# First attention of a two-block transformer kernel: each unit's transpositions placed ahead of the preceding unit's values on TensorE

## What is computed

```python
# "a": sparse attention, 8 heads of 64, 2 key/value heads; the keys of a query are chosen by an indexer
dots   = einsum('bqhd,bsd->bqhs', q_index, k_index)
iscore = einsum('bqh,bqhs->bqs', w_index, relu(dots))      # masked to the past, top 64 keys kept
p      = softmax(q_a @ k_a.T * scale, masked to the chosen keys);  o_a = p @ v_a
# "b": latent attention, 8 heads of 64 + 32 query/key features, 64 value features, causal
p      = softmax((q_nope @ k_nope.T + q_rope @ k_rope.T) * scale, masked);  o_b = p @ v_b
merged = sigmoid(g_a) * (o_a @ w_branch_a) + sigmoid(g_b) * (o_b @ w_branch_b)
h      = h + merged @ w_out
```

## Time and profile before

| | |
|---|---|
| three runs | 999.68, 1000.36, 1000.6 us; median 1000.36 us |
| the profiled execution | 999.73 us, of which 997.9 us are the span of the profile |
| granted TensorE clock over the span | 0.998 |
| busy, share of the span | PE 98%, weight loads 84%, DVE 68%, ACT 54%, POOL 4% |
| the chain that ended last | PE 76%, issue 19%, DVE 2%, others 1% each or less |
| first attention | units 0 to 15 from about 79.5 to 155.3 us |

### The profile page before, as it was taken

One profiled execution on the slowest core, in us unless ns is written; L12 is line 12 of the kernel. 1 busy time (PEld: TensorE's weight loads), 2 busy tenths in 40 slices (PEclk: granted clock), 3 DMA queues, 4 the chain that ended last, 5 costly groups with the idle time before them and its releaser, 6 DMA issues.

```text
span 997.9 us, 15646 instructions
## 1 busy us (share of the span) xinstructions
PE 981.6 (98%) x6349; PEld 841.6 (84%) x6349; DVE 677.7 (68%) x831; ACT 542.8 (54%) x708; POOL 42.9 (4%) x68
## 2 busy tenths in 40 slices
PE   7999999999999999999999999999999999999997
PEld 6887777898888888887889888888899898888885
DVE  5689787688777787777767565656656566555564
ACT  6676664476555565634445444444555455444452
POOL 1210000000000005000000000000000000000000
PEclk9999999999999999999999999999999999999999
DMA  8354335466656555844347565656553446656541
GB/s 306 103 192 158 109 120 178 161 211 211 209 170 209 171 168 164 261 146 155 120 133 259 188 207 190 204 185 201 185 168 133 155 142 214 207 172 207 174 163 43
DMA packets 121283, 175.89 MB, mean 176 GB/s; under 512 B 3167, under 2 KB 89770, under 8 KB 121226
## 3 DMA queue, kind: packets, MB, share of 16 engines
q1 hardware_dynamic: 118860, 168.82, 51.0%
q0 software_dynamic: 1600, 5.09, 1.6%
q10 hardware_dynamic: 766, 1.16, 0.5%
HBM read 173.82 MB, written 1.25 MB: 175 GB/s over the span
## 4 chain that ended last, share of the span: by engine, by line
PE 76%; issue 19%; DVE 2%; DMA 1%; ACT 1%; POOL 1%; SPq 0%; POOLq 0%; DVEq 0%; ACTq 0%
PE ps L1851 22%; PE ps L1901 16%; PE ps L1872 10%; PE ps L1900 7%; PE ps L1888 5%; PE ps L1915 3%; PE ps L1923 2%; DMA raw<-in_w_in 1%; PE ps L2141 1%; PE ps L2336 1%; PE ps L1903 1%; PE ps L1966 1%; PE ps L2169 1%; PE ps L2397 1%; PE ps L1997 1%
## 5 line engine op out<-in xcount | busy, mean ns | idle before, releaser
L1090 DVE TENSOR_TENSOR w_lo<-raw,w_hi 128x2048 fp32r<-128x2048 f32 (+3 forms) x153 | 345.3, 2261 | 125.2 <-ACT w_hi L548 124.9
L1901 PE MATMUL ps<-x_both,w_hi 128*128 128x512 f32 x992 | 342.7, 396 | 0.0
L548 ACT ACTIVATE w_hi<-raw 128x2048 fp32r<-128x2048 f32 (+3 forms) x161 | 302.4, 1879 | 58.9 <-PE ps L1851 40.1
L1900 PE MATMUL ps<-x_both,w_lo 128*128 128x256 f32 x868 | 242.0, 279 | 0.0
L1901 PEld LDWEIGHTS ps<-x_both,w_hi 128*128 128x128 f32 x992 | 179.1, 188 | 34.5
L1900 PEld LDWEIGHTS ps<-x_both,w_lo 128*128 128x128 f32 x868 | 163.6, 189 | 5.5
L803 ACT ACTIVATE work<-ps 128x512 f32<-128x512 f32 x66 | 39.3, 596 | 150.2 <-PE ps L1901 134.4
L1851 PE MATMUL ps<-w_hi,x_both 128*128 128x512 f32 (+1 forms) x320 | 101.5, 387 | 0.3 <-DVE w_lo L1090 0.3
L1851 PE MATMUL ps<-w_hi,hid_hi 128*128 128x512 f32 x240 | 93.8, 391 | 0.0
L1851 PE MATMUL ps<-w_hi,hid_lo 128*128 128x512 f32 x240 | 93.4, 389 | 0.0
L1851 PE MATMUL ps<-w_lo,hid_hi 128*128 128x512 f32 x240 | 93.4, 389 | 0.0
(11 more groups left out here) (294 smaller groups left out, 1274.2 us busy)
## 6 DMA issues: line engine op xcount, KB each, us to landing
raw<-in_ffn_w SPq DMA_DIRECT2D x66, 1024.0 KB, 5.1
raw<-in_w_up SPq DMA_DIRECT2D x22, 1024.0 KB, 5.1
raw<-in_hgrn_w_in SPq DMA_DIRECT2D x16, 1024.0 KB, 5.5
raw<-in_w_in SPq DMA_DIRECT2D x12, 1024.0 KB, 5.2
raw<-in_moba_w_in SPq DMA_DIRECT2D x12, 1024.0 KB, 5.2
raw<-in_w_down SPq DMA_DIRECT2D x11, 1024.0 KB, 5.0
raw<-in_w_out SPq DMA_DIRECT2D x4, 1024.0 KB, 5.1
raw<-in_hgrn_w_out SPq DMA_DIRECT2D x4, 1024.0 KB, 5.7
```

The source lines that it names most:

```text
L548: act.activation(w_hi[:, n % RING, 0:kc * cols], raw[:, n % RING, 0:kc * cols], ACT.Copy).then_inc(s["hi_ready"], 1)
L1090: dve.tensor_tensor(w_lo[:, n % RING, sl], raw[:, n % RING, sl], f32(w_hi[:, n % RING, sl]), ALU.subtract).then_inc(s["lo_ready"], 1)
L1900: pe.matmul(out[:, 0, :], w_lo[:, n % RING, at], x_hi[:, k, :], start=False, stop=False)
L1901: ins = pe.matmul(out, w_hi[:, n % RING, at], x_both[:, k, :, :], start=(k == 0), stop=(k == DC - 1))
```

## The change

In the first attention alone (`first == 0`) the values of unit u - 1 move behind the transpositions of unit u: PE's order in unit u becomes scores of u + 1, transpositions of u, values of u - 1, filler. Waits move with their instructions. The last value, after unit 15, stays where it is; so does everything on the other engines and in the second attention.

```diff
@@ -2130,7 +2130,7 @@
                 for u in range(first, first + count):
                     if u + 1 < first + count:
                         score(u + 1)
-                    if u > first:
+                    if u > first and first > 0:
                         value(u - 1)
                     pe.wait_ge(s["prob_ready"], u + 1)
                     if u >= first + 2:
@@ -2140,6 +2140,8 @@
                         for k in range(kt):
                             ins = pe.transpose(ps[:, u % 2, P * (kt * j + k):P * (kt * j + k) + P], buf[:, u % 2, j, P * k:P * k + P], ident)
                     ins.then_inc(s["probT_done"], 1)
+                    if u > first and first == 0:
+                        value(u - 1)
                     extra(u)
                 value(first + count - 1)
```

## The result

The changed kernel takes 1002.12 us (median of 16 runs), the kernel before, in 16 runs of the same series, 1000.05 us. The ratio is 1.0021 with a 95% interval of 1.0014 to 1.0028: slower by 2.07 us. The profiled execution took 1001.49 us with a span of 999.7 us. That is 1.8 us more span than before; the attention began 0.33 us earlier in this execution, in a part of the kernel that the change does not touch, so the part from there on is 2.1 us longer.

What follows compares the result with a forecast made beforehand. PE, busy 98% of the span, was taken as the bound. 6 x 0.04 + 0.10 + 7 x 0.20 + 0.40 = 2.14 us, added to 1000.36, gave 1002.5 us; range 1000.6 to 1003.8.

Steps and rivals of the forecast that it cites:

- Indexed units, +0.20: Units 7 to 14, first score to second filler matmul: four changes of form instead of three, 2.14 against 1.94 us.
- the dear case: Rival: transpositions to values take 0.63 us, as entry costs the 0.20 of leaving row form; +3.2 us, 1003.6; chance 0.16.
- Latent units, +0.04: Units 1 to 6: two changes of form before and after, 2.31 against 2.27 us; six units +0.24.
- Unit 2, +0.10 beside its 0.04: Transpositions in unit 2 lose the values' cover and wait for DVE's scaled probabilities: +0.10 us.
- Units 14 and 15, +0.40: Unit 15's transpositions wait for DVE's probabilities; +0.40 us for both together, unit 14's 0.20 disappearing in this wait.
- The free entry: Rival: transpositions run into the values without a drain, 0.42 us; +0.3 us, 1000.6; chance 0.19 together with no effect.
- the overlap on both sides: Rival: entering and leaving the values' column form are both free in 15 units; -2.3 us, 998.1; chance 0.07.
- PE might run ready matmuls ahead: Rival: PE runs ready matmuls ahead of waiting ones, so time stays; no chance of its own, counted with free entry.
- ACT and DVE at nothing: Transposed scores reach ACT about 0.6 us earlier, values' output about 0.5 later; cost put at nothing, uncovered up to 0.5.

Runs made afterwards that it cites:

- full-form runs: Old and new order with values computed in form 128*128: 1003.95 and 1003.86 us; both orders with indexed scores over all 128 rows instead: 1001.63 and 1002.73 us.
- unit 15 alone: New order in unit 15 only, old order elsewhere, against the kernel before: attention 76.13 us, +0.40; run once, its kernel time not used.
- first pairing: Old order, values of units u - 2 and u - 1 computed together in every odd unit from 3 on: 999.64 against 1000.01 us before, ratio 0.9995.
- second pairing: First pairing moved by one unit, pairs in even units, values of 14 and 15 at the end: 998.42 against 999.95 us before, ratio 0.9984.

## Why the prediction was right

**The forecast and the size.** +2.14 us was forecast, +2.07 measured in time and +2.22 in the trace's attention: 0.38 up to unit 6 (0.34 forecast), 1.45 in units 7 to 13 (1.40) and 0.39 from unit 14 on (0.40). The absolute 1002.5 stood 0.4 above the measured 1002.12, mostly because the three runs it started from had a median of 1000.36 and the 16 runs have 1000.05. The prediction had put its forecast on its own line of 2.0 us between slower and no change; with an interval of 1.4 to 2.8 us the loss is shown, but not on which side of that line it lies.

**Indexed units, +0.20.** Each term came within 0.01: 2.14, with 0.63, 0.59, 0.59 and 0.33 for the terms 0.63, 0.58, 0.59 and 0.34. The one step that no row of before showed, transpositions into column tiles, cost 0.58 to 0.59 (the dear case had 0.63, the free one 0.42), and the row it was taken from, the same length of records followed by a change of form, was the right neighbour. The split of that 0.58 was not right, and that the whole came out is in part luck. The prediction took 0.42 without a change of form and 0.16 for entering the column form. The runs have 0.44 for transpositions followed by full-form values, 0.05 more because these transpositions themselves stand behind the 64\*128 scores (0.49), and 0.09 to 0.10 for the entry. The same 0.09 to 0.10 shows at all three entries: 0.58 to 0.59 against 0.49, 0.53 against 0.44, and 0.96 against 0.86 from latent scores to values. The full-form runs show that the form is the cause and not the order: take away the values' form and the loss goes, take away the scores' form and 0.05 of an indexed unit's 0.20 remains. The Trainium skill (TensorEngine Tiling (Array Packing), Tiling Modes, Key Properties) states that a change of mode drains the engine. This rule gave the sign here, but not the size. With the 128 cycles that the Trainium skill puts on a drain in TensorE: Matmul & The Clock Gate, Part 2, the eight extra changes would be an estimated 0.4 us. The eight units lost 0.20 each. Where the count of changes stayed the same, in the latent units, the trace still has 0.05 a unit.

**Latent units, +0.04.** Measured +0.05: 0.87, 0.53, 0.59 and 0.33 for the terms 0.86, 0.52, 0.59 and 0.34.

**Unit 2, +0.10 beside its 0.04.** It took 2.44, +0.17 in all where 0.14 was forecast. One of the two waits for DVE in the trace is here.

**Units 14 and 15, +0.40.** Measured 0.40 (6.39 against 5.99), and the claim that unit 14's loss is not counted again was tested by itself: unit 15 alone gives the same 6.39 us.

**Rivals.** The free entry and the dear one are out by the term itself, 0.58 to 0.59 where they needed 0.42 and 0.63; the overlap on both sides is out by the 15 waits on entering and the 15 on leaving. That PE might run ready matmuls ahead is out: the records stand in the new program order.

**ACT and DVE at nothing.** Right for this change: no new wait for ACT appeared, and what follows the attention is within 0.1 us as long as before. The same assumption, made again for the first pairing, was wrong there: I had looked at the partners of the values and not at those of the filler, whose bank was being emptied under the values' cover.

## What to carry to other kernels

On a full PE, write down the form of the array of each group and count the changes: here each cost 0.1 to 0.2 us, and a reordering that neither adds nor removes an instruction added eight of them. Put groups with the same form together, even from different units of work. Then ask for every gap or group that you shorten which other engine's work it was covering; in the first pairing that was twice ACT's and once DVE's work on a bank of a product that has nothing to do with the attention.

## What the runs showed of the hardware

Behind a change of form the first weight load does not run ahead. In unit 7 of the changed kernel the loads of the values start with their first matmul, at 115.33, after 0.17 us of idle time; with full-form values in the same place they start at 116.13, under the transpositions and 0.11 ahead of the matmul at 116.24, without idle time:

```profile
115.33 0.42 PEld L2171 LDWEIGHTS ps<-work 128*64 128x64 f32 x8 [0.17 <-issue]
```

```profile
116.13 0.97 PEld L2171 LDWEIGHTS ps<-work 128*128 128x128 f32 x8
```

How much of a change's price is this late load and how much is PE itself was not separated; the cause of the price inside PE stays open.

Leaving the row form is paid in part by the first group behind it. Behind the 64\*128 scores, eight full-form value records took 0.99 us against 0.89 behind a full-form group, and four transpositions 0.49 against 0.44. I had taken a fixed price for each pair of forms, which was good to 0.05 us.

The 0.42 us from unit 0's transpositions to its filler, which I used as the price without any change of form, holds a small wait for ACT: the gate in front of that filler ended at 81.07 and the filler started at 81.12. With nothing to wait for it is 0.36, as in unit 1 of the second pairing:

```profile
85.55 0.60 PE L2149 MATMUL ps<-const,work 128*128 128x128 f32 x4
85.91 0.47 PE L1859 MATMUL ps<-w_hi,x_both 128*128 128x512 f32 x1
```

In the first pairing ACT's gate ended at 100.66 and the filler of unit 4 started at 100.70, 0.42 behind its transpositions, although no wait is named at that row. A start within 0.05 us of another engine's end may be a wait, named or not. That the 0.42 was still near the truth for the values was luck: full-form values follow the transpositions after 0.44, a filler after 0.36, so the distance without a change of form also depends on which group comes next.
